# Block sums of FFN weights made in place by adding transfers instead of by GpSimd, in the seven-product part of a diffusion-transformer layer on one core

## The reference

```python
    h2 = rmsnorm(x, norm2_g) * (1.0 + scale2) + shift2
    ffn = (jax.nn.silu(h2 @ w_ffn_gate) * (h2 @ w_ffn_up)) @ w_ffn_down
    x = x + gate2 * ffn
```

## Time and profile before

| what | value |
|---|---|
| time, median of 3 runs | 1331.96 us (1331.69 to 1333.9) |
| the profiled execution, its time | 1333.38 us |
| its span | 1331.7 us |
| granted TensorE clock, mean | 0.990 |
| PE / PEld busy | 1269.5 / 1159.1 us |
| DVE / ACT / POOL busy | 801.0 / 488.4 / 313.5 us |

### The profile page before, as it was taken

One profiled execution on the slowest core, in us unless ns is written; L12 is line 12 of the kernel. 1 busy time (PEld: TensorE's weight loads), 2 busy tenths in 40 slices (PEclk: granted clock), 3 DMA queues, 4 the chain that ended last, 5 costly groups with the idle time before them and its releaser, 6 DMA issues.

```text
span 1331.7 us, 19817 instructions
## 1 busy us (share of the span) xinstructions
PE 1269.5 (95%) x7734; PEld 1159.1 (87%) x7734; DVE 801.0 (60%) x1308; ACT 488.4 (37%) x812; POOL 313.5 (24%) x273
## 2 busy tenths in 40 slices
PE   5999999999999999998999899997999999999997
PEld 2798887799999999987788798887998899889986
DVE  4553112467566634372899654477873888558866
ACT  5352323353321222223677422344441344313434
POOL 1011000311011011111899400026400443005300
PEclk9999999999999999999899999999999999999999
DMA  9634231154344343452000224211323133222221
GB/s 312 193 111 119 63 95 48 40 159 142 112 158 148 122 110 98 128 187 94 1 1 2 81 79 174 64 32 32 95 95 95 32 95 96 95 63 63 88 88 79
DMA packets 87392, 129.56 MB, mean 97 GB/s; under 512 B 3529, under 2 KB 64450, under 8 KB 87186
## 3 DMA queue, kind: packets, MB, share of 16 engines
q1 hardware_dynamic: 76880, 95.17, 22.6%
q0 software_dynamic: 9104, 32.20, 7.9%
q10 hardware_dynamic: 1330, 1.10, 0.2%
HBM read 117.43 MB, written 4.73 MB: 92 GB/s over the span
## 4 chain that ended last, share of the span: by engine, by line
PE 74%; DVE 11%; POOL 6%; ACT 4%; issue 3%; DMA 1%; ACTq 0%; DVEq 0%
PE psum L421 30%; PE psum L458 27%; PE psum L664 10%; DVE seven_lo L694 5%; POOL probs L961 3%; POOL probs L967 3%; PE psum L407 1%; DVE hid L2158 1%; PE psum L1036 1%; PE psum L522 1%; PE psum L594 1%; DVE w_lo L390 1%; DVE partial L2188 1%; PE psum L1144 1%; DMA rows<-in_diff_subln_g 1%
## 5 line engine op out<-in xcount | busy, mean ns | idle before, releaser
L390 DVE TENSOR_TENSOR w_lo<-w_raw,w_hi 128x2048 fp32r<-128x2048 f32 x57 | 130.5, 2290 | 198.9 <-ACT w_hi L385 196.5
L385 ACT ACTIVATE w_hi<-w_raw 128x2048 fp32r<-128x2048 f32 x57 | 108.8, 1909 | 178.5 <-PE psum L458 107.6
L421 PE MATMUL psum<-h_hi,w_lo 128*128 128x320 f32 x672 | 154.6, 311 | 0.8 <-ACT y_nat L1486 0.8
L421 PE MATMUL psum<-h_hi,w_hi 128*128 128x320 f32 x672 | 153.1, 309 | 0.0
L421 PE MATMUL psum<-h_lo,w_hi 128*128 128x320 f32 x672 | 153.1, 309 | 0.0
L458 PE MATMUL psum<-w_hi,hid 128*128 128x512 f32 x440 | 135.6, 389 | 0.0
L421 PEld LDWEIGHTS psum<-h_hi,w_lo 128*128 128x128 f32 x672 | 111.8, 188 | 1.7 <-issue 1.7
L421 PEld LDWEIGHTS psum<-h_hi,w_hi 128*128 128x128 f32 x672 | 112.4, 188 | 0.0
L421 PEld LDWEIGHTS psum<-h_lo,w_hi 128*128 128x128 f32 x672 | 112.3, 188 | 0.0
L664 PE MATMUL psum<-h_hi,seven_lo 128*128 128x320 f32 x320 | 99.4, 311 | 4.4 <-DVE h_lo L2151 4.4
L684 ACT ACTIVATE seven_hi<-w_raw 128x512 fp32r<-128x512 f32 x100 | 61.9, 628 | 102.5 <-PE psum L664 70.6
(11 more groups left out here) (304 smaller groups left out, 2797.0 us busy)
## 6 DMA issues: line engine op xcount, KB each, us to landing
w_raw<-in_w_in SPq DMA_DIRECT2D x32, 1024.0 KB, 5.6
ada_b<-in_w_ada POOLq DMA_DIRECT2D x32, 512.0 KB, 4.0
w_raw<-in_w_ffn_gate SPq DMA_DIRECT2D x11, 1024.0 KB, 5.4
w_raw<-in_w_ffn_up SPq DMA_DIRECT2D x11, 1024.0 KB, 5.3
ada_a<-in_w_ada SPq DMA_DIRECT2D x8, 1024.0 KB, 13.2
w_raw<-in_w_ffn_down SPq DMA_DIRECT2D x8, 1024.0 KB, 5.1
w_raw<-in_w_ret_out SPq DMA_DIRECT2D x4, 1024.0 KB, 5.1
swapped<-qk_d POOLq DMA_DIRECT2D x32, 128.0 KB, 2.6
```

The lines of the kernel that those rows point to most:

```text
L385: act.activation(w_hi[s][:, :, :], w_raw[s][:, :, :], ACT.Copy).then_inc(w_hi_done, 1)
L390: dve.tensor_tensor(w_lo[s][:, :, :], w_raw[s][:, :, :], w_hi[s][:, :, :].bitcast(F32), ALU.subtract).then_inc(w_lo_done, 1)
L421: last = pe.matmul(bank(4 * par + 2 * j + h, HALF), w[:, k, cs], x[:, k, h * HALF:(h + 1) * HALF], start=(k == 0 and n == 0), stop=(k == K ...
```

## The change

The weight sums are no longer made by POOL's ALU. For each unit POOL now issues five transfers: a load of b12 from HBM into a tile of its own (`b12_copy`, one buffer), and four in-place adding transfers between tiles of SBUF, which read 256 KB, add it to 256 KB and write it back, 512 bytes at a time (4 runs in each of 128 partitions). So that all four are plain sums, signs are turned: two token sums are negated, and SiLU and the product of the hidden tiles take a factor of -1 for the second tile. The token sums are made by DVE. ACT makes T1's part before `finish_unit`, not behind; DVE makes the low parts of T1 behind its second group of adds, the low parts of the hidden tiles later; the last two adds of PSUM become one instruction.

```diff
-        t_sum = [at("t_sum0", B + 10, [P, KH, P]), at("t_sum1", W + 46, [P, KH, P])]
+        b12_copy = at("b12_copy", B + 10, [P, KH, P])
...
-            return (w[:, low_k, left], w[:, high_k, left], t_sum[0][:, :, :], w[:, high_k, right],
-                    t_sum[1][:, :, :], w[:, low_k, left], w[:, low_k, right])[p]
+            return (w[:, low_k, left], w[:, high_k, left], w[:, low_k, right], w[:, high_k, right],
+                    w[:, high_k, right], w[:, high_k, left], b12_copy[:, :, :])[p]
...
+                if n:
+                    pool.wait_ge(w_lo_done, unit)
+                pool.dma_start(b12_copy[:, :, :], matrix[:, low_k, c + P:c + UC]).then_inc(b12_in, 16)
                 pool.wait_ge(w_landed[par], (unit - par) * 8 + 16)
-                if n:
-                    pool.wait_ge(seven_l, (SEVEN - 1) * (n - 1) + T1 + 1)
-                pool.tensor_tensor(t_sum[0][:, :, :], b12, b11, ALU.subtract).then_inc(seven_T, 1)
-                pool.wait_ge(seven_T, 4 * n + T1_DONE)
-                pool.tensor_tensor(b12, b22, b12, ALU.subtract).then_inc(seven_T, 1)
-                if n:
-                    pool.wait_ge(seven_l, (SEVEN - 1) * (n - 1) + T2 + 1)
-                if (i, par) == (0, 0):
-                    pool.wait_ge(mm_done, 2 * unit + AHEAD)
-                pool.tensor_tensor(t_sum[1][:, :, :], b22, t_sum[0][:, :, :], ALU.subtract).then_inc(seven_T, 1)
-                pool.wait_ge(seven_T, 4 * n + T2_DONE)
-                pool.wait_ge(seven_l, (SEVEN - 1) * n + B11 + 1)
-                pool.tensor_tensor(b11, b21, t_sum[1][:, :, :], ALU.subtract).then_inc(seven_T, 1)
-
-            token_sums()
+                pool.dma_start(b12, b11, accum_op=ALU.add).then_inc(t_in[T1], 16)
+                pool.wait_ge(b12_in, 16 * (n + 1))
+                pool.dma_start(b12_copy[:, :, :], b22, accum_op=ALU.add).then_inc(t_in[T3], 16)
+                pool.wait_ge(t_in[T1], 16 * (n + 1))
+                pool.wait_ge(t_in[T3], 16 * (n + 1))
+                pool.wait_ge(seven_l, (SEVEN - 1) * n + B22 + 1)
+                pool.dma_start(b22, b12, accum_op=ALU.add).then_inc(t_in[T2], 16)
+                pool.wait_ge(t_in[T2], 16 * (n + 1))
+                pool.wait_ge(seven_l, (SEVEN - 1) * n + B21 + 1)
+                pool.dma_start(b21, b22, accum_op=ALU.add).then_inc(t_in[T4], 16)
+
+            pool.wait_ge(x1_done, 2 * TILES + AHEAD)
             for third in range(3):
                 for unit in units_of(third):
                     weight_sums(*unit)
...
-                prefill(0, (B11, B21, T1, B22), ready("up_first", 0, 0, 1))
+                prefill(0, (B11, B21), ready("up_first", 0, 0, 1))
                 for n in range(3):
                     high_of_token_sum(n)
+                prefill(0, (T1, B22), ready("up_first", 0, 0, 1))
...
                         act_seven(act, *following, B11)
-                    if previous:
-                        finish_unit(*previous)
                     copy_first(*unit)
                     if following:
                         act_seven(act, *following, B21)
                         act_seven(act, *following, T1)
+                    if previous:
+                        finish_unit(*previous)
+                    if following:
                         for p in (B22, T2, T4, T3):
                             act_seven(act, *following, p)
...
+            def token_sums():
+
+                x11, x21 = hf2[:, low_k, first_half], hf2[:, low_k, second_half]
+                x12, x22 = hf2[:, high_k, first_half], hf2[:, high_k, second_half]
+                dve.wait_ge(n2t["h2"]["lo"], 2 * KT)
+                dve.tensor_tensor(token_sum(0), x22, x21, ALU.subtract).then_inc(x_sum, 1)
+                dve.wait_ge(x_sum, 1)
+                dve.scalar_tensor_tensor(token_sum(1), token_sum(0), -1.0, x11, ALU.mult, ALU.subtract).then_inc(x_sum, 1)
+                dve.tensor_tensor(token_sum(2), x11, x21, ALU.subtract).then_inc(x_sum, 1)
+                dve.wait_ge(x_sum, 2)
+                dve.scalar_tensor_tensor(token_sum(3), x12, -1.0, token_sum(1), ALU.mult, ALU.subtract).then_inc(x_sum, 1)
...
                 dve.tensor_tensor(out[:, 0, first_half], partial[:, :], y, ALU.add).then_inc(seven_read, 1)
-                if pending:
-                    low_of_hidden(*pending)
                 if following:
-                    weights_low(following, (B11, B21, T1))
+                    weights_low(following, (B11, B21))
...
                 if following:
-                    weights_low(following, (B22, T2))
-                else:
+                    weights_low(following, (T1, B22, T2))
+                if pending:
+                    low_of_hidden(*pending)
+                if not following:
                     dve_split(dve, unit_of(f"down{third}", 0, 0), 0)
...
-                dve.tensor_tensor(out[:, 1, second_half], partial[:, :], z, ALU.add).then_inc(freed["dve"], 1)
-                dve.tensor_tensor(out[:, 0, second_half], partial[:, :], y, ALU.add).then_inc(freed["dve"], 1)
+                dve.tensor_tensor(out[:, :, second_half], partial[:, :].unsqueeze(1).to_broadcast([P, 2, HALF]), T_tile(4 * par + 1),
+                                  ALU.add).then_inc(freed["dve"], 2)
```

More of the change, by code:

```diff
@@ L112 @@
 SEVEN = 7
+SIGN = (1.0, -1.0)
 B11, B21, T1, B22, T2, T4, T3 = range(SEVEN)
-T1_DONE, T3_DONE, T2_DONE, T4_DONE = 1, 2, 3, 4
 SETUP_ACT, SETUP_DVE = 14, 8
@@ L371, in build @@
         hid_h, hid_l = sem("hid_h"), sem("hid_l")
-        seven_T, seven_h, seven_l, seven_mm = sem("seven_T"), sem("seven_h"), sem("seven_l"), sem("seven_mm")
+        b12_in = sem("b12_in")
+        t_in = {T1: sem("t1_in"), T2: sem("t2_in"), T3: sem("t3_in"), T4: sem("t4_in")}
+        seven_h, seven_l, seven_mm = sem("seven_h"), sem("seven_l"), sem("seven_mm")
         seven_read, silu_done, hid_m = sem("seven_read"), sem("silu_done"), sem("hid_m")
@@ L675, in act_seven @@
             act.wait_ge(w_landed[par], (unit - par) * 8 + 16)
-            if p in (T1, T2, T3, T4):
-                act.wait_ge(seven_T, 4 * n + {T1: T1_DONE, T2: T2_DONE, T3: T3_DONE, T4: T4_DONE}[p])
+            if p in t_in:
+                act.wait_ge(t_in[p], 16 * (n + 1))
             if after is not None:
@@ L980, in _ @@
             pool.dma_start(x1[:, LAT_TILES, :], a["x_prompt"][0]).then_inc(ld_x1, 16)
[L982 to L992, removed]
             def weight_sums(third, i, par):
@@ L999, in weight_sums @@
                 b21, b22 = w[:, high_k, 0:P], w[:, high_k, P:UC]
-                pool.wait_ge(w_landed[par], (unit - par) * 8 + 16)
-                if n:
-                    pool.wait_ge(seven_l, (SEVEN - 1) * (n - 1) + T1 + 1)
-                pool.tensor_tensor(t_sum[0][:, :, :], b12, b11, ALU.subtract).then_inc(seven_T, 1)
-                pool.wait_ge(seven_T, 4 * n + T1_DONE)
-                pool.tensor_tensor(b12, b22, b12, ALU.subtract).then_inc(seven_T, 1)
-                if n:
-                    pool.wait_ge(seven_l, (SEVEN - 1) * (n - 1) + T2 + 1)
-                if (i, par) == (0, 0):
-                    pool.wait_ge(mm_done, 2 * unit + AHEAD)
-                pool.tensor_tensor(t_sum[1][:, :, :], b22, t_sum[0][:, :, :], ALU.subtract).then_inc(seven_T, 1)
-                pool.wait_ge(seven_T, 4 * n + T2_DONE)
-                pool.wait_ge(seven_l, (SEVEN - 1) * n + B11 + 1)
-                pool.tensor_tensor(b11, b21, t_sum[1][:, :, :], ALU.subtract).then_inc(seven_T, 1)
-            token_sums()
+                matrix = a["w_ffn_up" if par else "w_ffn_gate"][0].rearrange("(k p) c -> p k c", p=P)
+                c = UC * (HID_BASE[third] + first_tile(third, i)) // 2
+                if n:
+                    pool.wait_ge(w_lo_done, unit)
+                pool.dma_start(b12_copy[:, :, :], matrix[:, low_k, c + P:c + UC]).then_inc(b12_in, 16)
+                pool.wait_ge(w_landed[par], (unit - par) * 8 + 16)
+                pool.dma_start(b12, b11, accum_op=ALU.add).then_inc(t_in[T1], 16)
[9 more added lines that the diff above has]
+            pool.wait_ge(x1_done, 2 * TILES + AHEAD)
             for third in range(3):
@@ L1625, in finish_unit @@
                         act.wait_ge(freed["dve"], freed_after(f"up{third}", i, 0, 1 - j))
-                        act.activation(silu_g[:, j, :], silu_g[:, j, :], ACT.Silu).then_inc(silu_done, 1)
+                        act.activation(silu_g[:, j, :], silu_g[:, j, :], ACT.Silu, scale=SIGN[j]).then_inc(silu_done, 1)
                 else:
@@ L2158, in low_of_hidden @@
                     dve.tensor_tensor(hid_lo[:, k, :], hid_f[:, j, :], hid_hi[:, k, :].bitcast(F32), ALU.subtract).then_inc(hid_l, 1)
+            def token_sums():
[8 more added lines that the diff above has]
+                dve.scalar_tensor_tensor(token_sum(3), x12, -1.0, token_sum(1), ALU.mult, ALU.subtract).then_inc(x_sum, 1)
             def first_pair():
-                weights_low((0, 0, 0), (B11, B21, T1, B22))
```

(10 more changed lines are left out.)

## The result

The change makes the kernel slower: **1480.28 us** (median of 4 runs, 1478.66 to 1482.2) against 1332.63 us, a ratio of 1.1108 with a 95% interval of 1.1089 to 1.1127. The direction was forecast, the size was not: 1398 us and a range up to 1460.

The account below looks back on a forecast made before the run. TensorE was taken to set the pace, 12.3 us a unit, until serial transfers made it 17.8. Up phases of 29.7 + 302.6 = 332.3 us against 266.5 added 65.8, giving 1398 us, range 1342 to 1460.

Parts of the forecast that it names:

- the chain: Up phases: each unit's transfers wait for the previous unit's last low part, then run serially; 17.8 us a unit.
- The term of b12's load: Start of each unit: 0.75 us issue, then landing priced at 3.8 us like the other transfers.
- X: The moment a unit's last low part, T3's, is done; the next unit's five transfers may not be issued before it.
- L: Distance from one unit's X to the next in the up phases: 6.4 + 3D, forecast 17.8 us.
- D: Time of one transfer of this size from issue to landing: 3.8 us taken; 51 us of total time per microsecond.
- case 1: Forecast case: the chain with D from 3.3 to 4.4 us, L 16.3 to 19.6, 1371 to 1428 us; chance 0.46.
- Handovers: Passing from one step of the chain to the next: 0.1 us each, counted within L.
- both ways into T2's transfer: Through T1 and B22's low part, 4.2 + D; through b12's load and T3's transfer, 2D + 0.2.
- case 2: Adding much dearer than copying: D from 4.4 to 5.4 us or somewhat past; at 5.4, 1479 us; chance 0.27.
- The length of a phase by L: The three up phases together: 29.7 + 17L, 332.3 us against 266.5 before.
- The fixed part: 29.7 us of the up phases: time to each third's first X, plus 5.1 us behind each last one.
- The 20 us to be won: TensorE's gaps in the up phases, all taken as gone without POOL's ALU work and with earlier token sums: -20 us.

Follow-up runs that it names:

- the first experiment: The changed kernel, with SP issuing its 1 MB w_raw load only once the b12 load of the same moment has landed: 1483.6 us.
- the half-size run: The changed kernel with each adding transfer made over only two of the four 512-byte runs per partition, 128 KB: 1429.6 us.
- three reorderings tried: Changed kernel with two b12 tiles, 1424.2 us; then also b12 load ahead of T2's transfer, 1410.5; then also T1's and B22's low parts ahead of adds, 1374.9.

## Why the prediction came out as it did

- **What bounds the kernel, and the chain**: right. The added time lies in the up phases, TensorE waits once a unit ahead of its T2 product for `copy_first`, the low parts take 689 ns on the mean of 120, and POOL's b12 load waits for the last low part in all 17 units that were said to be in the chain.
- **The term of b12's load**: this failed most. The prediction wrote that "The next w_raw load, issued at the same X, shares the DMA engines with the first two transfers", and then priced both at 3.8 like the others. Measured: 6.0 us for b12 and 6.4 for T1. That is 2.2 us of the 4.5 by which L fell short, and the first experiment shows that it is this sharing.
- **D**: 3.8 forecast, 4.2 measured, undisturbed. Three in the chain after b12's: 1.2 us. The range of case 1 (3.3 to 4.4) held it.
- **Handovers**: 0.1 us each in the sum; POOL's next issue came 0.3 to 0.5 us after a landing (4.74 and 4.46 between issues of transfers of 4.2), and 0.3 after the last low part. About 1.1 us are left for them.
- **The longer of two ways**: the prediction gave both ways into T2's transfer and put them level at D near 4, but its L = 6.4 + 3D follows the way through T1 for every D. Above D = 4 the other is longer and L is 2.4 + 4D: 19.2 at the measured 4.2, and 24.0 instead of 22.6 at the 5.4 of case 2, which makes its time 1503 us and not 1479.
- **The length of a phase by L**: the slope held. 17 units of the chain took 22.3 us each on the mean, 379.3 of the 416.1 us; the half-size run lost 2.9 us a unit and 51 us in all. The fixed part came to 36.8 us instead of 29.7: 1.5 us more ahead of the first X, and 7.0 instead of 5.1 us behind the last X of each third. These tails are the clock, which the forecast left out: their 36 weight loads take 6.7 to 7.0 us instead of 5.1, at a granted clock of 0.71 to 0.76. In the unit of the timeline above it shows best. Ahead of the gap it is granted fully, behind it at half, in windows at 1100, 1113.5 and 1117 us:

```profile
1100.00:1106.00 6.00, 6.00 (x43) 6.00 (x42) 0.92 (x2) 0.11 (x1) 1.28 (x1) 1.00 0.68 77
...
1113.50:1117.00 3.50, 3.47 (x13) 3.50 (x14) 1.60 (x3) 0.40 (x1) 2.08 (x2) 0.50 0.69 202
1117.00:1120.00 3.00, 3.00 (x18) 3.00 (x17) 1.47 (x3) 0.00 (x0) 0.11 (x1) 0.78 1.21 278
```

  0.50 is the lower of TensorE's two levels, 1.2 GHz instead of 2.4. Weight loads there start 0.27 us apart, against 0.147. Inside a unit the wait for the chain hides this; at the end of each third it lengthens the tail.
- **The sum again with measured terms**: 17 x 22.31 + 36.8 = 416.1, less 266.5 is 149.6, where 65.8 was forecast. Of the difference of 83.8, 76.7 come from L (37 from b12's load, 20 from D, 19 from the handovers) and 7.1 from the fixed part. The prediction's up phases "of about 104, 133 and 98 us" should read 101 for the first by its own sum; measured were 128.6, 167.0 and 120.5.
- **The range**: it treated D as the only uncertain term. With D from 3.3 to 4.4, the longer way and 2.2 us for the sharing, case 1 would have given about 1410 to 1473 us; the handovers and the clock make up the rest. Case 2 has a time near the one measured (1479), but by a mechanism that isn't there: D was 4.2, not 5.4.
- **The rule of a fixed 2.0 us and the bytes over 436 GB/s** in the Trainium skill, "DMA: Bandwidth & Descriptors", section on the anatomy of a DMA on the GpSimd path: the estimate of 2.6 us agrees with the plain copy's 2.7, and I was wrong to hold the row of 3.6 against it; that row is a median over pairs issued together. For the adding transfer it is 1.6 us too low. That adding is dearer for its second read (the Trainium skill, "Collectives: The Full Stack", the bandwidth ceiling) points the right way, 2.7 to 4.2, but by an estimate from both pages, with only the moved 0.6 us doubled, it would be 3.2.
- **The 20 us to be won, and where the gaps were**: the prediction laid the 1.35 us at 1057.70 before T1's product and named T1 of the first unit as what the token sums delay by 4.6 us. By the count of weight loads, 12 to a product, the gap at 1057.70 is ahead of T3's, as are nine more of the 13, and the 4.6 us are ahead of B22's product, which waits for the low part of the last token sum: the cause was right, the place was not. Ahead of T3, TensorE waits for DVE's second add of PSUM. In the changed kernel these gaps are gone, as forecast. But a kernel in which all gaps are gone was never run: with the transfers out POOL's ALU is back, so are gaps ahead of T3's product, and all the rest of the change gives 7.1 us. That the full 20 can be had is not shown.

## What to carry to other kernels

A transfer in a serial chain costs its landing time plus a handover, and more if a large load starts at the same event: look at what else the releasing semaphore starts, and price the first transfers under it. Before work goes from an ALU to DMA, add up the engine time of the transfers against the unit of the bounding engine; here 3.3 us a unit became 13.2 by an estimate from shares, with 12.3 for TensorE, and none of the three reorderings tried came back to the kernel before. And if a change bundles a mechanism with reorderings, run the reorderings alone: here they were worth 7 us, where the token sums on DVE alone gave 4.3. The fastest median, 1322.7 us, is the changed kernel without its transfers, with two b12 tiles and the hidden low parts last.

## What the runs showed of the hardware that was not expected

- An adding transfer between SBUF tiles, 256 KB in runs of 512 bytes, holds POOL for 1.28 us at its issue, a plain one for 0.75; half the adding still for 1.18. The time at issue hardly goes by the amount, the time to landing does (3.1 and 4.2 us).
- With three adding transfers issued one behind the other, 0.75 us apart, the records of the issue instructions overlap and get longer: 1.3, 1.8 and 2.4 us at the median in the run with the b12 load ahead of T2.
- Beside POOL's additions two low parts of DVE took 2.97 us, against 1.29 us without (128x512 each).
- Beside a 1 MB load a transfer took 2.6 to 2.7 us longer, the same for a load from HBM (3.4 to 6.0) and for an adding transfer within SBUF (4.2 to 6.9).
